# Key scores head by head beside the query projections, and expert numbering split by picks, in a one-core transformer layer

## What is computed

```
def peer(h, w_q, sub_k1, sub_k2, u, v):
    q = (h @ w_q).reshape(B, S, PEER_HEADS, 2, PEER_HALF)
    s1 = jnp.einsum('bshd,nd->bshn', q[..., 0, :], sub_k1).astype(jnp.float32)
    s2 = jnp.einsum('bshd,nd->bshn', q[..., 1, :], sub_k2).astype(jnp.float32)
    v1, i1 = lax.top_k(s1, PEER_TOPK)
    v2, i2 = lax.top_k(s2, PEER_TOPK)
    cand = (v1[..., :, None] + v2[..., None, :]).reshape(B, S, PEER_HEADS, PEER_TOPK * PEER_TOPK)
    cidx = (i1[..., :, None] * PEER_KEYS + i2[..., None, :]).reshape(B, S, PEER_HEADS, PEER_TOPK * PEER_TOPK)
    sc, pos = lax.top_k(cand, PEER_TOPK)
    eidx = jnp.take_along_axis(cidx, pos, axis=-1)
    gate = jax.nn.softmax(sc, axis=-1)
...
    act = jax.nn.gelu(jnp.einsum('td,thkd->thk', hx, u[ex]))
    return jnp.einsum('thk,thkd->td', (gx.astype(act.dtype) * act), v[ex])
```

## Time and profile before

| | before |
| --- | --- |
| median of three runs | 1827.28 us |
| profiled execution, and its span | 1828.94, 1827.1 us |
| PE busy | 1672.7 us (92%) |
| DVE busy | 1118.8 us (61%) |
| ACT busy | 326.5 us (18%) |
| POOL busy | 614.4 us (34%) |
| moved by DMA | 475.56 MB, mean 260 GB/s |
| dots L989 | 256, 304.6 us |
| gathers of u rows L484 | 256, 250.7 us |
| dense products L1411 | 2048 passes, 447.5 us |

### The profile page before, as it was taken

One profiled execution on the slowest core, in us unless ns is written; L12 is line 12 of the kernel. 1 busy time (PEld: TensorE's weight loads), 2 busy tenths in 40 slices (PEclk: granted clock), 3 DMA queues, 4 the chain that ended last, 5 costly groups with the idle time before them and its releaser, 6 DMA issues.

```text
span 1827.1 us, 17662 instructions
## 1 busy us (share of the span) xinstructions
PE 1672.7 (92%) x6294; PEld 1088.2 (60%) x6294; DVE 1118.8 (61%) x2409; ACT 326.5 (18%) x857; POOL 614.4 (34%) x650
## 2 busy tenths in 40 slices
PE   6988999999998999999997996667999999999795
PEld 3454454455884888888886885556444444444342
DVE  0010444431219999999947567999666555566794
ACT  3002444340111021111111113554000000000032
POOL 0000345430002244333335443222545334444570
PEclk9988999999999999999998998777999999999897
DMA  6222111024446799999999998333999999999991
GB/s 205 80 93 93 57 36 35 12 90 144 139 146 199 254 344 373 362 357 378 344 369 349 409 409 319 112 115 100 401 409 409 409 409 409 409 410 409 408 348 54
DMA packets 131972, 475.56 MB, mean 260 GB/s; under 512 B 14716, under 2 KB 15740, under 8 KB 131885
## 3 DMA queue, kind: packets, MB, share of 16 engines
q0 software_dynamic: 73728, 268.47, 38.4%
q1 hardware_dynamic: 58156, 205.97, 30.2%
HBM read 471.19 MB, written 3.19 MB: 260 GB/s over the span
## 4 chain that ended last, share of the span: by engine, by line
PE 49%; DMA 30%; DVE 14%; issue 3%; POOL 2%; ACT 1%; SPq 1%; ACTq 0%; DVEq 0%; POOLq 0%
DMA arena<-in_v,eidx 21%; PE psum L1411 17%; DMA arena<-in_u,eidx 7%; PE psum L1319 6%; PE psum L1258 6%; PE psum L1148 5%; PE psum L1291 3%; PE psum L1279 3%; DVE arena L1011 3%; DVE arena L989 3%; DVE arena L1043 2%; DVE arena L1046 2%; DVE arena L1020 2%; PE psum L1216 2%; PE psum L1370 2%
## 5 line engine op out<-in xcount | busy, mean ns | idle before, releaser
L1411 PE MATMUL psum<-arena 128*128 128x256 f32 x2048 | 447.5, 382 | 13.3 <-issue 12.5
L484 POOL DMA_INDIRECT arena<-in_u,eidx x256 | 250.7, 979 | 595.3 <-DVE dots L989 369.0
L1429 PE MATMUL psum<-arena 128*128 128x512 f32 x1024 | 440.4, 592 | 2.2 <-DMA arena<-in_vd 1.4
L1411 PEld LDWEIGHTS psum<-arena 128*128 128x128 f32 x2048 | 391.6, 191 | 68.7 <-issue 14.0
L1011 DVE SCALAR_TENSOR_TENSOR arena<-arena,wts 128x1024 f32<-128x1024 f32 x254 | 323.3, 1285 | 175.2 <-DMA arena<-in_v,eidx 168.8
L484 POOL DMA_INDIRECT arena<-in_v,eidx x256 | 256.4, 1002 | 288.9 <-DVE arena L1011 233.0
L989 DVE CUSTOM_DVE_ANT_0 arena<-psum,arena 128x1024 f32<-128x1024 f32 x256 | 304.6, 1221 | 61.2 <-DMA arena<-in_u,eidx 50.8
L1429 PEld LDWEIGHTS psum<-arena 128*128 128x128 f32 x1024 | 194.2, 190 | 247.2 <-issue 243.0
L463 POOL TENSOR_SCALAR arena<-arena 128x256 f32<-128x256 f32 (+4 forms) x128 | 105.9, 846 | 281.5 <-DVE arena L767 223.9
L1422 PE MATMUL psum<-arena 128*128 128x128 f32 x512 | 100.7, 366 | 58.7 <-DVE arena L1046 36.5
L1422 PEld LDWEIGHTS psum<-arena 128*128 128x128 f32 x512 | 90.2, 266 | 69.3 <-DVE arena L1046 59.0
(11 more groups left out here) (167 smaller groups left out, 1274.4 us busy)
## 6 DMA issues: line engine op xcount, KB each, us to landing
arena<-in_ut SPq DMA_DIRECT2D x128, 512.0 KB
arena<-in_vd SPq DMA_DIRECT2D x128, 512.0 KB
arena<-in_wpack SPq DMA_DIRECT2D x105, 512.0 KB, 3.6
arena<-in_u,eidx POOLq DMA_INDIRECT x256
arena<-in_v,eidx POOLq DMA_INDIRECT x256
arena<-in_w_pg SPq DMA_DIRECT2D x8, 512.0 KB
arena<-in_x SPq DMA_DIRECT2D x4, 512.0 KB, 4.9
arena<-bias_rows SPq DMA_DIRECT2D x8, 256.0 KB, 5.6
```

Source lines behind the costliest of these rows:

```text
L484: G.indirect_dma_start(out=row_slot(n), out_offset=None, in_=a["v"] if values else a["u"], in_offset=bass.IndirectOffsetOnAxis(ap=eidx[:, ...
L1411: last = T.matmul(ps[6 + c % 2][:, 0:DT], u[:, k * P:(k + 1) * P], h2T1[:, k, :], start=(k == 0), stop=(k == KC - 1))
L1429: last = T.matmul(ps[BANK + 2 * t + h], mixed[:, c, t * P:(t + 1) * P], stream[:, c % SRING, h * HALF:(h + 1) * HALF], start=(c == 0), sto ...
```

## The change

PE: the key scores of a head are made for both tiles of the pass, right behind the next head's query products, in banks 6 and 7; the queries use banks 4 and 5. `scores(0)` to `scores(3)` go. ACT copies out accordingly. DVE: `top_of_halves` takes one head of both tiles of a pass. For tiles 0 and 1 all eight heads come ahead of the first pick of pairs; for tiles 2 and 3 they stand between the dots. Candidate order is changed so that the 20 candidates that can be among the eight best come first (`LOW_RUNS`); the first eight picks are compared with these 20 for four heads at a time (640 elements), the last eight with all 50 for two heads at a time (800 elements). The position numbers for this are copied once, near the program's start, into `candno`. Gathers and dots go by `PICK_ORDER`: picks 1 to 8 of heads 0 to 3, of heads 4 to 7, then picks 9 to 16. The exponentials of the gates come after chunks 40 and 56 for tiles 2 and 3, and ahead of chunk 0 for tiles 0 and 1.

```diff
 
+LOW_RUNS = [(0, 1, 0, 8), (1, 1, 0, 4), (2, 2, 0, 2), (4, 4, 0, 1)]
...
+HIGH_RUNS = [(0, 1, 8, 16), (1, 1, 4, 8), (2, 1, 2, 5), (3, 1, 2, 4), (4, 1, 1, 3), (5, 3, 1, 2), (8, 8, 0, 1)]
+NLOW = sum(na * (b1 - b0) for _, na, b0, b1 in LOW_RUNS)
+ROW_LEN = [nb for _, na, nb in RUNS for _ in range(na)]
+ROW_START = [sum(ROW_LEN[:r]) for r in range(TK)]
+PICK_ORDER = [h * TK + k for h0, h1, k0 in ((0, 4, 0), (4, 8, 0), (0, 8, 8)) for h in range(h0, h1)
+              for k in range(k0, k0 + 8)]
...
             def gather(n):
                 values, k = divmod(n, NG * COLS)
+                col = k // COLS * COLS + PICK_ORDER[k % COLS]
                 if n == 0:
                     pool.wait_ge(merged, 2 * KC)
                     pool.wait_ge(experts_known, 1)
-                if n == TK:
-                    pool.wait_ge(experts_known, 2)
+                if n == 4 * 8:
+                    pool.wait_ge(experts_known, 3)
                 if n == COLS:
-                    pool.wait_ge(experts_known, 3)
+                    pool.wait_ge(experts_known, 4)
...
             peer_norm(0, 2)
             turned_evac(h2T0, 0)
-            query_evac(0)
-            score_evac(0)
+            heads_evac(0)
             peer_norm(2, 4)
-            score_evac(1)
             turned_evac(h2T1, 1)
-            query_evac(1)
-            score_evac(2)
-            score_evac(3)
+            heads_evac(1)
             gate_exp(0)
+            gate_exp(1)
...
             for c in range(CHUNKS):
                 if c == 8:
-                    act.wait_ge(experts_known, 2)
-                if c in (64, 72, 80):
-                    act.wait_ge(halves_done, (c - 64) // 8 + 1)
-                if c == 96:
+                    act.wait_ge(experts_known, 3)
+                if c == 64:
                     act.wait_ge(split_ready, 2)
                 if c == 120:
                     act.wait_ge(dot_rows_ready, 2)
                 act.wait_ge(dense_scores, c + 1)
                 A.activation(mixed[:, c, :], ps[6 + c % 2][:, 0:DT], ACT.Gelu_apprx_tanh).then_inc(dense_gelu, 1)
-                if c == 24:
-                    gate_exp(1)
+                if c == 40:
+                    gate_exp(2)
                 if c == 56:
-                    gate_exp(2)
-                if c == 88:
                     gate_exp(3)
...
             V.memset(rbias[0:HEADS, 2 * P - 1:S + P], NEG).then_inc(bias_rows_out, 1)
+            dve.wait_ge(pool_consts_set, 6)
+            off = 0
+            for a0, na, b0, b1 in LOW_RUNS + HIGH_RUNS:
+                for x in range(na):
+                    start = ROW_START[a0 + x]
+                    V.tensor_copy(candno[:, off:off + b1 - b0], iota[:, start + b0:start + b1])
+                    off += b1 - b0
             dve.wait_ge(rms_ready, 1)
...
-            def top_of_halves(t, j0, j1):
-
-                sc = s12[t]
-                rest = scratch(t).rearrange("p (j n) -> p j n", n=PK)
-                dve.wait_ge(keyscores_out, 4 * t + j1 // 4)
-                for j in range(j0, j1):
-                    last = V.max(vals[:, j, 0:8], sc[:, j, :])
+            def top_of_halves(h, p):
+
+                dve.wait_ge(keyscores_out, 2 * (PH * h + p) + 2)
+                rest = scratch(2 * h).rearrange("p (j n) -> p j n", n=PK)
+                rows = [(vals[t], idxu[t], s12[2 * h + t], 2 * p + x, 2 * t + x) for t in range(2) for x in range(2)]
+                for v, i, sc, j, r in rows:
+                    last = V.max(v[:, j, 0:8], sc[:, j, :])
                 after(last)
...
-                for src, dst in ((v4, cand), (i4, cidx)):
+                whole = [(a0, na, 0, nb) for a0, na, nb in RUNS]
+                for src, dst, runs in ((v4, cand, whole), (i4, cidx, LOW_RUNS + HIGH_RUNS)):
                     off = 0
-                    for a0, na, nb in RUNS:
+                    for a0, na, b0, b1 in runs:
+                        nb = b1 - b0
                         d = dst[:, :, off:off + na * nb].rearrange("p h (x y) -> p h x y", x=na)
                         last = V.tensor_tensor(d, src[:, :, 0, a0:a0 + na].unsqueeze(3).broadcast_to([P, PH, na, nb]),
-                                               src[:, :, 1, 0:nb].unsqueeze(2).broadcast_to([P, PH, na, nb]), ALU.add)
+                                               src[:, :, 1, b0:b1].unsqueeze(2).broadcast_to([P, PH, na, nb]), ALU.add)
...
-            def number_experts(t, h0, h1):
-
-                eq = scratch(t)[:, 0:TK * NCAND].rearrange("p (k c) -> p k c", k=TK)
-                for h in range(h0, h1):
-                    after(V.tensor_tensor(eq, iota50.unsqueeze(1).broadcast_to([P, TK, NCAND]),
-                                          posf[:, h, :].unsqueeze(2).broadcast_to([P, TK, NCAND]), ALU.is_equal))
-                    after(V.tensor_tensor(eq, eq, cidx[:, h, :].unsqueeze(1).broadcast_to([P, TK, NCAND]), ALU.mult))
-                    after(V.tensor_reduce(esel[:, h, :], eq, AX.X, ALU.add))
-
-            def publish(t, h0, h1):
-
-                V.tensor_copy(eidx[:, t * COLS + h0 * TK:t * COLS + h1 * TK],
-                              esel[:, h0:h1, :].rearrange("p h k -> p (h k)")).then_inc(experts_known, 1)
+            def number_experts(t, h0, h1, k0, n):
+
+                nh = h1 - h0
+                eq = scratch(t)[:, 0:nh * 8 * n].rearrange("p (h k c) -> p h k c", h=nh, k=8)
+                shape = [P, nh, 8, n]
+                after(V.tensor_tensor(eq, candno[:, 0:n].unsqueeze(1).unsqueeze(1).broadcast_to(shape),
+                                      posf[:, h0:h1, k0:k0 + 8].unsqueeze(3).broadcast_to(shape), ALU.is_equal))
+                after(V.tensor_tensor(eq, eq, cidx[:, h0:h1, 0:n].unsqueeze(2).broadcast_to(shape), ALU.mult))
+                after(V.tensor_reduce(esel[:, h0:h1, k0:k0 + 8], eq, AX.X, ALU.add))
+
+            def number_low(t, half):
+                number_experts(t, 4 * half, 4 * half + 4, 0, NLOW)
...
+            def number_high(t, pair):
+                number_experts(t, 2 * pair, 2 * pair + 2, 8, NCAND)
...
-            for c in range(4):
-                top_of_halves(0, 4 * c, 4 * c + 4)
-            pair_up()
+            for p in range(PH):
+                top_of_halves(0, p)
+            pair_up(0)
             top_pairs(0)
+            number_low(0, 0)
+            publish(0, 0, 4, 0, 8)
             add_mixer(2)
             add_mixer(3)
-            number_experts(0, 0, 1)
-            publish(0, 0, 1)
-            number_experts(0, 1, 2)
+            number_low(0, 1)
+            number_high(0, 0)
             peer_norm(2, 4)
-            number_experts(0, 2, PH)
-            publish(0, 1, PH)
+            for pair in range(1, 4):
+                number_high(0, pair)
+            publish(0, 4, 8, 0, 8)
+            publish(0, 0, 8, 8, 16)
...
+                col = PICK_ORDER[k]
...
+            def later_top(t, step):
+                if step == 0:
+                    pair_up(t)
+                if step == 1:
                     top_pairs(t)
-                if k in (20, 24, 28, 32):
-                    number_experts(t, (k - 20) // 2, (k - 20) // 2 + 2)
-                if k == 34:
+                if step == 2:
+                    number_low(t, 0)
+                    number_low(t, 1)
+                if step == 3:
+                    number_high(t, 0)
+                    number_high(t, 1)
+                if step == 4:
+                    number_high(t, 2)
+                    number_high(t, 3)
                     if t < NG:
-                        publish(t, 0, PH)
+                        publish(t, 0, PH, 0, TK)
                     else:
                         split(t)
...
             for k in range(COLS):
                 dot(0, k)
-                for t in range(1, TILES):
-                    later_top(t, k - 2 - 42 * (t - 1))
-                if k == 20:
+                step, off = divmod(k, 4)
+                if off == 2 and step < 5:
+                    later_top(1, step)
+                if off == 2 and 5 <= step < 13:
+                    top_of_halves(1, step - 5)
+                if off == 2 and 13 <= step < 18:
+                    later_top(2, step - 13)
+                if off == 2 and 18 <= step < 23:
+                    later_top(3, step - 18)
+                if k == 40:
                     gates(0)
-                if k == 62:
                     gates(1)
-                if k == 104:
+                if k == 96:
                     gates(2)
...
+            def scores(h, p):
+                pe.wait_ge(query_out, PH * h + p + 1)
+                if PH * h + p >= 2:
+                    pe.wait_ge(keyscores_out, 2 * (PH * h + p) - 2)
+                for t in range(2):
+                    for jj in range(2):
+                        last = T.matmul(ps[6 + p % 2][:, (2 * t + jj) * PK:(2 * t + jj + 1) * PK],
```

(22 more changed lines are left out.)

94 lines of the change are left out of this document (42 added, 52 removed).

## The result

The changed kernel takes 1803.89 us, the kernel before 1827.28 on the same chip: a ratio of 0.9867, 95% interval 0.9850 to 0.9885, 23.4 us less. The profiled execution took 1803.86 us with a span of 1802.1; before it was 1828.9 with 1827.1. The forecast of 1808.3 had the direction right, and that PE's last chunk takes over from DVE as the later one. Its gain (19.0 us) was 4.4 us too small, and the time lies 0.9 us above the low end of the range (1803).

A forecast was written before the change was run, and what follows sets the result against it. The later of PE's last dense chunk and DVE's 96th dot bounds the kernel, DVE before, PE after: 655.4 + 442.9 = 1098.3, + 3 + 0.1 = 1101.4 instead of 1120.45; 1827.3 - 19.0 = 1808.3 us, range 1803 to 1826.

The forecast's parts named there:

- Start, +1.3: Program start: 24 small DVE copies ahead of the first norm take 1.8 us, of which 1.3 us delay stays.
- queries with scores, 63.5 each: PE's query products with key scores per pass: 55.5 + 7.2 for eight score steps + 0.8 for a wait.
- Start of the dense stage, +2.2: PE's dense stage starts 2.2 us later, at 655.4, from +1.3 + 1.4 - 0.5.
- Dots from 597.6, last routing step at 828: DVE: dots start at 597.6 instead of 603.73 us; the last routing step between them comes at 828 us.
- DVE's stand gone: Dense stage: DVE's 23.8 us wait for ACT's exponential of tile 3's gates disappears.
- Saturated dots 2.03 us each, 96th dot at 1094: Behind 828 us DMA limits DVE to 2.03 us per dot; tile 1's 96th dot comes at 1094 us.
- Rival (c): Before the one-hots: saturated dots take 2.15 us, DVE stays later, ending at 1109; gain 11, 1816 us; chance 0.13.
- Stalls of PE, +3: Dense stage: PE loses 3 us waiting for blocks behind runs of gathers, within bounds 0 and 17.6.
- (a): Dense stage: one PE stall episode costs all 17.6 us, PE ends at 1115.9; gain 4.5, 1822.8 us; chance 0.15.
- (b): Dense stage: gathers starve PE's dense stream repeatedly; two episodes give 35 us, 1840 us, slower; chance 0.12.
- First one-hot: Start of DVE's one-hot stage: at 1101.4 us (1098.3 + 3 + 0.1) instead of 1120.45, so -19.0 us.
- The rival in which the saturated queues slow PE's stream: Dense stage: DVE's gathers, asked for without pause, starve PE's dense blocks again and again; slower, chance 0.12.

The follow-up runs named there:

- the second one: The kernel before, unchanged, profiled once more: 1827.2 us.
- With the stand back: The changed kernel with tile 3's gate exponential put back from behind dense chunk 56 to behind chunk 88: 1827.43 us, ratio 0.9995 to the kernel before.

## Why the prediction was right or wrong

- **The bound, and its exchange.** Right that DVE's 96th dot set the end before and PE's last chunk would after. The margin before was not the kernel's: 6.7 us in the trace that I read, some 24 us in the second one.
- **Start, +1.3.** Right: the copies took 1.55 us, where 1.8 was forecast, queries(0) began 1.37 us later, and PE's second block ran without its 0.51 us of waiting. The Trainium skill (VectorE: DVE Perf Modes, on the TRN2 errata) has a fixed cost of about 150 cycles for each instruction; the estimate of 3.8 us by it is not borne out by these copies.
- **queries with scores, 63.5 each. This term was mis-sized.** 62.56 in the first pass, 62.73 in the second. The eight score steps took 7.04 us (7.2 forecast), and the wait for the last evacuation (0.73) isn't there: from 547.19 PE runs head 6's scores and then head 7's, and ACT has the last queries out by 547.99, before head 7's begin.
- **Start of the dense stage, +2.2. This step failed, by 1.7 us.** turn(1) came at 585.84, where I had 1.3 + 1.4 = 2.7 us more than before and found 1.75; behind it the queries took 63.47 us to the dense stage, where I had 64.2. Both shortfalls, 0.9 and 0.7, are the term above, once in each pass: project_out(1) started at 549.03 where 549.9 was due. The sum is +0.46. (In it, 64.2 for 64.8 is -0.6 and not -0.5.)
- **Numbering operations, 2.6 and 3.1 for three.** Right: 640 elements 0.82 each, 800 elements 0.99.
- **Dots from 597.6, last routing step at 828.** 596.27 and 827.98. The working from step to step held over 230 us.
- **DVE's stand gone.** Right: 0 us after. The prediction took it as one term of several. With the stand back, all the others together were worth nothing.
- **Saturated dots 2.03 us each, 96th dot at 1094.** 1091.7. Between 900 and 1050 us DVE made 73 dots, 2.05 us each. The 3 us for a copy and gates were not to be added: DVE stands idle at nearly every dot there, and without them the sum is 1091. DVE waits 5.0 us for PE, where 4 was forecast without the stall term and 7 with it. Rival (c) falls.
- **Stalls of PE, +3. This step failed, by 3.0 us.** They were 0. I had read one execution's loss as a response to DVE's stand, and priced a return of it. In the thirteen other traces of this record, three of them with stands of 23.5 to 45.6 us, PE made its chunks without a stall. Without it there was no ground for rivals (a) and (b), 0.27 of the chances, which made the upper half of the range. The low end was drawn as the case without a stall and with 2 us off the copies and the low halves. These came near their forecast, and the 1.7 us came off queries with scores instead, so that the low end fits so closely is partly luck.
- **First one-hot.** 1.7 + 3.0 = 4.7 us are the whole difference between 1101.4 and 1096.70, and that again nearly the whole one between 1808.3 and 1803.9.
- **Third and fourth stage follow whole.** Right within a microsecond (152.7 for 153.5, 552.7 for 553.2, counted from the values' first product; my 157 and 550 cut them at another place).
- **The rival in which the saturated queues slow PE's stream.** 408 to 409 GB/s for 225 us and PE busy 20.00 of 20: a dense block of 0.524 MB came every 3.455 us all the time. From the round-robin rule of the Trainium skill (DMA: Bandwidth & Descriptors, section Queues, rings and completion order) I had worked out that no stall would come, and the sum by it, 3 us less, was the better one. This trace agrees with it (no stall at 408 to 409 GB/s), but that the queues take turns no run shows, and the window 980 to 1000, with PE busy 9.84 us at 410 GB/s, is one in which PE did lack blocks while SP's queue waited for something remote.

## What to carry to other kernels

Where an engine works in program order, look at what its small operations are queued behind: ACT's exponential behind a chunk's gelu tied DVE to PE's count of chunks, and until it moved, two edits that took some 42 us of work off DVE (21.6 + 20.8) were worth 0. Before a stall gets a price of its own, see it in a second trace; the end of the stage (here 1120.45 and 1119.92) tells whether it was on the path at all. And where a stage has a fixed number of bytes to fetch, count the transfer time that stays unused: a microsecond of an engine is worth what it takes off that. Here it was 21.4 of 25.4 us in one place, 8.5 of 21.6 and 10.2 of 20.8 in others.
